# Output projection of a hybrid decoder step in two passes over the tokens, with the router's steps for the first 128 tokens inside the second pass

## The chip, the core and the metric

The kernel runs on one core of a Trainium2 chip. The core has TensorE (matrix products, written PE in the profile, its weight loads PEld), VectorE (DVE), ScalarE (ACT), GpSimd (POOL) and SyncE (SP), which here only issues transfers to 16 DMA engines. The engines run their own instruction streams and wait for each other on semaphores. The metric is the time of one execution on the device, in microseconds.

## What is computed

One inference step of a one-layer decoder trunk for 256 prompt tokens and 8 sampled tokens, 264 in all, width 1024: two recurrent branches, merged and projected by w_out, and then a mixture of 32 experts of which each token takes 4. All arithmetic is in 32-bit floats. What matters here is the end of the mixer and the mixture:

```python
merged = jax.nn.sigmoid(g_a) * branch_a + jax.nn.sigmoid(g_b) * branch_b
x = x + merged @ w_out                       # 1024 x 1024
u = rmsnorm(x, norm_ffn)
logits = u @ w_router + b_router             # 32 experts
top_v, top_i = lax.top_k(logits, TOP_K)      # TOP_K = 4
gates = jax.nn.softmax(top_v, axis=-1)
# for each expert e and its tokens xb:
gu = xb @ w_gate_up[e] + b_gate_up[e]        # 1024 x 2048
act = (up + 1.0) * (gate * jax.nn.sigmoid(SWIGLU_ALPHA * gate))
y = act @ w_down[e] + b_down[e]              # 1024 x 1024
```

The first two lines are written together here from the surrounding step; the rest is the reference's own. An expert has 12 MB of weights, all 32 have 384 MB (403 million bytes), and each is loaded once.

## The kernel before

**Layout.** Activations lie transposed: `xT` holds x as 8 tiles (`KT`) of 128 rows of the model width by 264 tokens. The tokens also come in three row tiles, `ROWS` = 128, 128 and 8 (the 8 sampled ones), called tile 0, 1 and 2 below. PSUM has eight banks, `ps[0]` to `ps[7]`; names such as `p_u`, `p_parts`, `p_logits` and `p_early` are the same eight banks in other roles.

**Output projection.** `project` (L1079) makes one output tile of 128 rows after the other. The w_out tiles are its last eight: 8 matmuls (k) of 128 x 128 weights against 264 columns, into `ps[0]` or `ps[1]` in turn. A matmul of this kind shows as two records in the trace, so a tile is 16 records. Its end raises `acc_ready` (89 to 96 for the w_out tiles; 88 marks the end of w_proj_b). VectorE adds the tile to `xT` (L1731) and raises `acc2_emptied`, for which TensorE waits before it uses that bank again. w_out lies in the four slots of `stream`, 256 columns each, and each slot is filled when w_proj_b's tile in it is done.

**Router.** TensorE forms partial products of `w_router` with `xT` (`logits_of`, four at a time side by side in the array, into `p_parts`) and turns `xT` into rows of tokens (`turn_u(t, h, js)`: token tile t, half h of the width, into `p_u`). ScalarE squares these rows (`square_u`, L790), takes the root (`root_u`, L797) and scales them (L809, `u_taken`). VectorE copies the partial products (L1765), TensorE sums them per token (`p_logits`), and VectorE runs, per token tile, scale and bias (L1743), the eight largest (L1745), cut to four (L1746, L1747), and the mark of chosen experts (L1752). From the marks, TensorE counts each token's rank at its expert (`p_rank0` for tile 0; `p_rank12` for tiles 1 and 2), VectorE makes a slot number (L1757) and a selection matrix `pick` (L1761), and TensorE gathers the first experts' inputs with it (`gather`). `keep_busy` is filler: matmuls whose results nobody reads.

**Experts.** They go in 16 pairs. A pair has six units of weights: four for gate and up, two for down, 4 MB each. There are five places for units in on-chip memory (`unit[0]` to `unit[4]`); place 3 is the memory of the four w_out slots, place 2 is free from `acc_ready` 88 on. SyncE issues the loads in the order of use; before it overwrites a place, it waits for `w_used`, which TensorE raises by one for each half unit (two k) that it has used. Ahead of the experts, SyncE's queue stands as in these lines, followed by the loads that wait for `w_used`:

```python
            sp.wait_ge(S["acc_ready"], 88)
            load_unit(0, 2, 2)
            sp.wait_ge(S["acc_ready"], 92)
            load_half(0, 3, 3, 0, unit_landed[3])
            sp.wait_ge(S["acc_ready"], 96)
            load_half(0, 3, 3, 1, half_landed[3])
            load_half(0, 4, 4, 1, half_landed[4])
```

The order of the work is written out by hand in each engine's block. Functions in the listing are those that the change touches and their callers.

## Time and profile before

| | us |
|---|---|
| median of 3 runs | 1379.17 (1378.71 to 1382.08) |
| the profiled execution | 1380.69 |
| its span in the trace | 1378.9 |
| TensorE busy, whole span | 1341.8 (97%) |
| VectorE busy | 417.9 (30%) |
| ScalarE busy | 260.3 (19%) |
| GpSimd busy | 38.9 (3%) |

By stretch of the span:

| stretch, us | what | TensorE busy | DMA share | GB/s |
|---|---|---|---|---|
| 325 to 415 | w_proj_a, w_proj_b | 89.87 of 90 | 0.82 | 259 |
| 415 to 457.5 | w_out, router | 40.95 of 42.5 | 0.81 | 325 |
| 457.5 to 1365 | experts | 883.28 of 907.5 | 0.99 | 422 |
| 1365 to 1378.9 | last sums, output | 7.21 of 13.9 | 0.21 | 78 |

The profile is one execution of the program. Busy time of matmuls includes modelled ends and so reaches over small gaps; where the spacing of matmuls matters, starts of successive rows are the better measure. The granted clock of TensorE was full (1.00) in most windows. A high busy share of TensorE and a DMA share of 0.99 stand side by side in the experts' stretch, so the shares alone don't say which one sets the pace.

### The profile page before, as it was taken

The page shows a single profiled execution, that of the slowest core. Times are in us where ns is not written, and L with a number is a line of the kernel's source. Part 1 is how long each engine was busy: PE and PEld are TensorE (multiplying, and loading weights), DVE is VectorE, ACT ScalarE, POOL GpSimd, SP SyncE. Part 2 cuts the span into 40 slices and gives each one's busy share as a digit, 9 for nine tenths or more (in the row PEclk, how much of TensorE's full clock was granted, in tenths as well). Part 3 has the DMA queues.
Part 4 walks back from the last instruction along what each step waited for, and adds up shares of the span by engine and source line. Part 5 has one row for each costly group of instructions (what it writes and reads, how often), then busy time and mean ns, then how long its engine had stood idle before and what let it go on. Part 6 is the DMA issues. An engine that isn't in the chain of part 4 may idle for free.

```text
span 1378.9 us, 16760 instructions
## 1 busy us (share of the span) xinstructions
PE 1341.8 (97%) x6864; PEld 746.5 (54%) x6864; DVE 417.9 (30%) x1089; ACT 260.3 (19%) x589; POOL 38.9 (3%) x58
## 2 busy tenths in 40 slices
PE   9999999999999999999999999999999989999998
PEld 8888878888888443443434444434334333434443
DVE  3754555887312321221122121211211211212112
ACT  2113273476200310110101101101011010101102
POOL 1000011210000000000000000000000000000000
PEclk9999999999999999999999999999999999999999
DMA  9444546898797899999999999999999999999995
GB/s 249 125 150 137 155 154 218 272 334 311 216 322 287 327 411 412 436 429 429 433 429 429 433 431 429 432 431 429 433 431 426 436 429 426 437 428 432 433 421 200
DMA packets 92549, 488.93 MB, mean 355 GB/s; under 512 B 8403, under 2 KB 72107, under 8 KB 76935
## 3 DMA queue, kind: packets, MB, share of 16 engines
q1 hardware_dynamic: 83560, 460.46, 82.6%
q0 software_dynamic: 4608, 24.41, 5.0%
q10 hardware_dynamic: 4306, 2.98, 0.8%
q8 instruction: 56, 0.92, 0.3%
q14 instruction: 19, 0.16, 0.0%
HBM read 476.91 MB, written 11.19 MB: 354 GB/s over the span
## 4 chain that ended last, share of the span: by engine, by line
PE 74%; DMA 21%; ACT 3%; DVE 1%; issue 0%; ACTq 0%; POOLq 0%; POOL 0%; SPq 0%; DVEq 0%
PE bank L310 72%; DMA ring<-in_w_gate_up 9%; DMA ring<-in_w_down 9%; DMA plain_conv<-in_w_down 3%; PE bank L914 2%; ACT ring L715 0%; ACT plain_conv L639 0%; ACT ring L677 0%; ACT ring L670 0%; DVE ring L1565 0%; DVE exn L1565 0%; ACT ring L665 0%; ACT ring L663 0%; DVE plain_conv L1562 0%; DVE ring L1562 0%
## 5 line engine op out<-in xcount | busy, mean ns | idle before, releaser
L310 PE MATMUL bank<-ring,plain_conv 128*64 128x512 f32 x1280 | 296.4, 605 | 7.6 <-DMA ring<-in_w_gate_up 7.6
L310 PE MATMUL bank<-exn,ring 128*128 128x264 f32 (+1 forms) x1168 | 265.9, 389 | 2.5 <-ACT plain_conv L611 2.3
L310 PEld LDWEIGHTS bank<-exn,ring 128*128 128x128 f32 (+1 forms) x1168 | 220.3, 190 | 44.6 <-issue 3.6
L310 PE MATMUL bank<-plain_conv 128*64 128x512 f32 (+2 forms) x848 | 186.7, 581 | 9.2 <-DMA plain_conv<-in_w_gate_up 8.8
L310 PEld LDWEIGHTS bank<-ring,plain_conv 128*64 128x64 f32 x1280 | 91.6, 139 | 187.3 <-issue 172.3
L310 PE MATMUL bank<-ring,exn 128*64 128x512 f32 x576 | 127.6, 595 | 3.3 <-DMA ring<-in_w_down 3.3
L310 PEld LDWEIGHTS bank<-plain_conv 128*64 128x64 f32 (+1 forms) x848 | 63.0, 140 | 123.8 <-issue 107.3
L1806 DVE TENSOR_TENSOR xT<-xT,bank 128x264 f32<-128x264 f32 x128 | 55.0, 430 | 222.7 <-PE bank L310 221.0
L1812 DVE TENSOR_SCALAR bank<-bank 128x512 f32<-128x512 f32 x31 | 21.7, 700 | 316.7 <-PE bank L310 316.7
L310 PE MATMUL bank<-plain_conv,exn 128*64 128x512 f32 (+1 forms) x422 | 99.9, 590 | 1.2 <-DMA plain_conv<-in_w_down 0.9
L823 ACT ACTIVATE exn<-bank 128x512 f32<-128x512 f32 x31 | 18.5, 598 | 413.8 <-DVE bank L1812 413.8
L310 PEld LDWEIGHTS bank<-rstd,exn 128*128 128x128 f32 (+2 forms) x772 | 76.9, 190 | 15.9 <-issue 13.0
L310 PE MATMUL bank<-rstd,exn 128*128 128x128 f32 (+2 forms) x772 | 83.7, 280 | 0.2 <-DVE rstd L1761 0.2
L310 PEld LDWEIGHTS bank<-ring,exn 128*64 128x64 f32 x576 | 40.2, 137 | 77.3 <-issue 72.1
L310 PE MATMUL bank<-ring 128*128 128x264 f32 (+3 forms) x520 | 80.4, 336 | 0.0
L310 PEld LDWEIGHTS bank<-ring 128*128 128x128 f32 (+1 forms) x520 | 67.8, 170 | 13.3 <-issue 4.8
L828 ACT COPY exn<-bank 128x512 f32<-128x512 f32 x31 | 18.2, 587 | 256.6 <-PE bank L914 250.3
L310 PEld LDWEIGHTS bank<-plain_conv,exn 128*64 128x64 f32 (+1 forms) x422 | 31.4, 137 | 59.6 <-issue 56.5
L310 PE MATMUL bank<-rstd,plain_conv 128*128 128x264 f32 x256 | 61.2, 392 | 0.0
L310 PEld LDWEIGHTS bank<-rstd,plain_conv 128*128 128x128 f32 x256 | 47.3, 190 | 20.3 <-issue 13.0
L310 PE MATMUL bank<-plain_conv,ring 128*128 128x264 f32 x256 | 57.8, 387 | 0.1
L1693 DVE TENSOR_TENSOR plain_conv<-bank,small 128x512 f32<-128x512 f32 x15 | 10.4, 692 | 146.6 <-PE bank L310 146.6
(294 smaller groups left out, 865.3 us busy)
## 6 DMA issues: line engine op xcount, KB each, us to landing
ring<-in_w_gate_up SPq DMA_DIRECT2D x35, 4096.0 KB, 38.0
plain_conv<-in_w_gate_up SPq DMA_DIRECT2D x23, 4096.0 KB, 39.8
ring<-in_w_down SPq DMA_DIRECT2D x16, 4096.0 KB, 39.2
plain_conv<-in_w_down SPq DMA_DIRECT2D x11, 4096.0 KB, 37.5
ring<-in_w_in SPq DMA_DIRECT2D x36, 1024.0 KB, 5.3
ring<-in_w_gate_up SPq DMA_DIRECT2D x8, 2048.0 KB, 10.9
ring<-in_w_down SPq DMA_DIRECT2D x5, 2048.0 KB, 9.1
ring<-in_w_proj_b SPq DMA_DIRECT2D x8, 1024.0 KB, 8.8
```

The source lines that it names most:

```text
L310: return nc.tensor.matmul(out, w, x, start=start, stop=stop)
L823: nc.scalar.activation(h_act, gate, ACT.Sigmoid, scale=1.702).then_inc(S["sg_ready"], 1)
L828: nc.scalar.copy(to.rearrange("p c s -> p (c s)"), bank[:, :]).then_inc(S["ht_ready"], 1)
L914: return nc.tensor.transpose(out, src, ident[0:k, 0:k])
L1693: done("xt_left", V.tensor_tensor(xt[:, 0:4, :], bank[:, :].rearrange("p (k s) -> p k s", k=4), n_ffn_x[:, 0:4].unsqueeze(2).to_broadcast( ...
L1806: done("comb_emptied", V.tensor_tensor(xT[:, c, :], xT[:, c, :], p_comb[c % 4][:, 0:NT], ALU.add))
L1812: V.tensor_scalar(g_last if last else gate, gate, 7.0, None, ALU.min).then_inc(S["g1_ready"], 1)
```

## The change

w_out's eight output tiles are made twice (`project_out(u)`, u = 0 to 15): in pass one over the first 128 tokens, in pass two over the other 136. `acc_ready` and `acc2_emptied` count eight more. `logits_of` takes a column range. Tile 0's router steps (partial products, turns, squares, root, logits, mark, ranks, pick, scaling) stand between the tiles of pass two on TensorE, VectorE and ScalarE; after pass two, tiles 1 and 2 go through the same steps, written in pairs. Some PSUM roles move to other banks. The gather of tile 0 for the first experts stands ahead of the ranks of tiles 1 and 2, one of the two filler blocks is gone, the other stands behind that gather. SyncE waits for `acc_ready` 100 and 104 where it waited for 92 and 96. The cut diff:

```diff
@@ -285,7 +285,7 @@
-        p_parts, p_logits, p_rank0, p_rank12, p_early = ps[5], ps[0], ps[1], ps[2], ps[0]
+        p_parts, p_logits0, p_logits, p_rank0, p_rank12, p_early = ps[5], ps[4], ps[1], ps[7], ps[2], ps[0]
@@ -394,9 +394,9 @@
             load_half(0, 4, 4, 0, unit_landed[4])
             sp.wait_ge(S["acc_ready"], 88)
             load_unit(0, 2, 2)
-            sp.wait_ge(S["acc_ready"], 92)
+            sp.wait_ge(S["acc_ready"], 100)
             load_half(0, 3, 3, 0, unit_landed[3])
-            sp.wait_ge(S["acc_ready"], 96)
+            sp.wait_ge(S["acc_ready"], 104)
             load_half(0, 3, 3, 1, half_landed[3])
...
@@ -786,29 +786,39 @@
...
+            square_u(0, 0)
+            square_u(0, 1)
+            root_u(0)
+            scale_u(0, 0)
+            scale_u(0, 1)
+            square_u(1, 0)
+            square_u(2, 0)
+            for t in range(1, 3):
                 square_u(t, 1)
                 root_u(t)
             for h in range(2):
-                for t, n in enumerate(ROWS):
-                    act.wait_ge(S["rstd_ready"], t + 1)
-                    scaled = u_tok[t][0:n, 512 * h:512 * h + 512] if t < 2 else us[32 * h:32 * h + n, :]
-                    nc.scalar.activation(scaled.rearrange("n (s p) -> n s p", s=4),
-                                         p_u[t][h][0:n, :].rearrange("n (p s) -> n s p", s=4), ACT.Copy,
-                                         scale=rstd_u[0:n, t:t + 1]).then_inc(S["u_taken"], 1)
+                for t in range(1, 3):
+                    scale_u(t, h)
...
+            def project_out(u):
+
+                half, t = u // KT, u % KT
+                cols = other_cols if half else first_cols
+                if half == 0 and t % 2 == 0:
+                    pe.wait_ge(landed[t // 2], 16 * 12 + 16)
+                pe.wait_ge(S["acc2_emptied"], KT - 1 + u)
+                for k in range(KT):
+                    if u == 0:
+                        pe.wait_ge(S["merged_ready"], k + 1)
+                    w = stream[t // 2][:, 256 * k + P * (t % 2):256 * k + P * (t % 2) + P]
+                    ins = mm(ps[u % 2][:, cols], w, plain[:, GA + k, cols], k == 0, k == KT - 1)
+                ins.then_inc(S["acc_ready"], 1)
+
             pe.wait_ge(emptied["s"], sum(w == "s" for _, w in uses))
             pe.wait_ge(emptied["v"], sum(w == "v" for _, w in uses))
-            for t in range(KT):
-                project(12, KT, lambda k: plain[:, GA + k, :], 16, t, t + 1, ready=lambda k: (S["merged_ready"], k + 1))
-                if t == 5:
-                    pe.wait_ge(S["acc2_emptied"], KT + 4)
-                    pe.wait_ge(S["router_set"], 2)
-                    logits_of(range(4))
-                    for w in range(3):
-                        turn_u(w, 0, range(4))
-            pe.wait_ge(S["acc2_emptied"], 2 * KT - 1)
-            turn_u(0, 1, range(3))
-            turn_u(1, 1, range(3))
+            for u in range(KT + 1):
+                project_out(u)
             pe.wait_ge(S["acc2_emptied"], 2 * KT)
-            turn_u(0, 1, [3])
-            logits_of(range(4, KT)).then_inc(S["parts_filled"], 1)
-            turn_u(1, 1, [3])
+            pe.wait_ge(S["router_set"], 2)
+            logits_of(range(KT), first_cols).then_inc(S["parts_filled"], 1)
+            turn_u(0, 0, range(4))
+            project_out(KT + 1)
+            turn_u(0, 1, range(4))
             pe.wait_ge(S["parts_taken"], 1)
-            for t, n in enumerate(ROWS):
-                ins = mm(p_logits[0:n, E * t:E * t + E], parts[:, P * t:P * t + n], one_of[:, 0:E], True, True)
-            ins.then_inc(S["logits_filled"], 1)
-            turn_u(2, 1, range(4))
-            keep_busy(p_rank0, 2)
+            turn_logits(p_logits0, [0])
+            for u in range(KT + 2, KT + 5):
+                project_out(u)
             pe.wait_ge(S["mark_ready"], 1)
             mm(p_rank0[:, 0:E], before[:, :], mark[:, 0, :], True, True).then_inc(S["rank0_filled"], 1)
+            project_out(KT + 5)
+            pe.wait_ge(S["acc2_emptied"], 2 * KT + 4)
+            logits_of(range(4), other_cols)
+            for w in range(1, 3):
+                turn_u(w, 0, range(4))
+            for u in range(KT + 6, 2 * KT):
+                project_out(u)
+            pe.wait_ge(S["pick0_ready"], 1)
+            pe.wait_ge(S["acc2_emptied"], 3 * KT - 1)
+            turn_u(1, 1, range(3))
+            pe.wait_ge(S["acc2_emptied"], 3 * KT)
+            turn_u(1, 1, [3])
+            logits_of(range(4, KT), other_cols).then_inc(S["parts_filled"], 1)
+            pe.wait_ge(S["parts_taken"], 2)
+            turn_logits(p_logits, (1, 2))
+            turn_u(2, 1, range(4))
             pe.wait_ge(S["u_taken"], 2)
-            keep_busy(p_first[0], 2)
-            pe.wait_ge(S["mark_ready"], 2)
-            mm(p_rank12[:, 0:E], ones[:, :], mark[:, 0, :], True, False).then_inc(S["fin_filled"], 5)
-            mm(p_rank12[:, 0:E], before[:, :], mark[:, 1, :], False, True)
-            mm(p_rank12[0:TS, E:2 * E], ones[:, 0:TS], mark[:, 0, :], True, False)
-            mm(p_rank12[0:TS, E:2 * E], ones[:, 0:TS], mark[:, 1, :], False, False)
-            mm(p_rank12[0:TS, E:2 * E], before[0:TS, 0:TS], mark[0:TS, 2, :], False, True).then_inc(S["rank12_filled"], 1)
 
...
-            pe.wait_ge(S["u_taken"], 3)
-            for t in range(3):
+            gather(p_early, range(2), [0])
+            keep_busy(p_rank12, 2)
+            pe.wait_ge(S["mark_ready"], 2)
+            mm(p_rank12[:, 0:E], ones[:, :], mark[:, 0, :], True, False).then_inc(S["fin_filled"], 5)
+            mm(p_rank12[:, 0:E], before[:, :], mark[:, 1, :], False, True)
+            mm(p_rank12[0:TS, E:2 * E], ones[:, 0:TS], mark[:, 0, :], True, False)
+            mm(p_rank12[0:TS, E:2 * E], ones[:, 0:TS], mark[:, 1, :], False, False)
+            mm(p_rank12[0:TS, E:2 * E], before[0:TS, 0:TS], mark[0:TS, 2, :], False, True).then_inc(S["rank12_filled"], 1)
+            pe.wait_ge(S["u_taken"], 4)
+            for t in range(1, 3):
                 pe.wait_ge(S["pick0_ready"], t + 1)
                 ins = gather(p_early, range(2), [t])
             ins.then_inc(S["early_filled"], 1)
@@ -1726,24 +1767,38 @@
...
-            for t in range(KT):
-                dve.wait_ge(S["acc_ready"], 88 + t + 1)
-                V.tensor_tensor(xT[:, t, :], xT[:, t, :], ps[t % 2][:, 0:NT], ALU.add).then_inc(S["acc2_emptied"], 1)
-                if t == KT - 2:
-                    for w, n in enumerate(ROWS):
-                        dve.wait_ge(S["usq_ready"], w + 1)
-                        done("part_ready", V.tensor_scalar(ssq_p[0:n, w:w + 1], ssq_h[0:n, w, 0:1], 1.0 / D, EPS, ALU.mult, ALU.add))
-
+            def add_out(u):
+
+                cols = slice(P, NT) if u >= KT else slice(0, P)
+                dve.wait_ge(S["acc_ready"], 88 + u + 1)
+                V.tensor_tensor(xT[:, u % KT, cols], xT[:, u % KT, cols], ps[u % 2][:, cols], ALU.add).then_inc(S["acc2_emptied"], 1)
...
@@ -1761,18 +1816,47 @@
...
+            for u in range(KT + 1):
+                add_out(u)
             dve.wait_ge(S["parts_filled"], 1)
-            done("parts_taken", V.tensor_copy(parts, p_parts[:, 0:NT]))
+            done("parts_taken", V.tensor_copy(parts[:, 0:P], p_parts[:, 0:P]))
+            add_out(KT + 1)
+            mean_square(0, 1)
+            add_out(KT + 2)
+            token_scale(0)
+            dve.wait_ge(S["rstd_ready"], 1)
             dve.wait_ge(S["logits_filled"], 1)
-            link(token_logits(0))
+            link(token_logits(0, p_logits0))
+            link(token_top(0))
+            add_out(KT + 3)
+            link(V.memset(top[:, 0, TOPK:8], LOWEST))
+            link(token_left(0))
             mark_tokens(0, 1)
-            link(token_logits(1))
-            link(token_logits(2))
-            mark_tokens(1, 2)
-            dve.wait_ge(S["mark_ready"], 2)
+            add_out(KT + 4)
             dve.wait_ge(S["rank0_filled"], 1)
             link(place_tokens(0, p_rank0[:, 0:E]))
             pick_first(0)
+            for u in range(KT + 5, 2 * KT - 1):
+                add_out(u)
+            mean_square(1, 3)
+            mean_square(2, 4)
+            add_out(2 * KT - 1)
+            dve.wait_ge(S["parts_filled"], 2)
+            done("parts_taken", V.tensor_copy(parts[:, P:NT], p_parts[:, P:NT]))
+            token_scale(1)
+            dve.wait_ge(S["rstd_ready"], 2)
+            dve.wait_ge(S["logits_filled"], 2)
+            link(token_logits(1, p_logits))
+            link(token_top(1))
+            token_scale(2)
+            dve.wait_ge(S["rstd_ready"], 3)
+            link(token_logits(2, p_logits))
+            link(token_top(2))
+            link(V.memset(top[:, 1:3, TOPK:8], LOWEST))
+            token_left(1)
+            link(token_left(2))
+            mark_tokens(1, 2)
+            dve.wait_ge(S["mark_ready"], 2)
             dve.wait_ge(S["rank12_filled"], 1)
             place_tokens(1, p_rank12[:, 0:E])
             place_tokens(2, p_rank12[0:TS, E:2 * E])
```

What stands in a row on the engines shows the same at three places. The rows give the line, the operation, the result and what it is made of, and its size as rows by columns. On TensorE w_out's matmuls are those on plain_conv,ring; those on xT,exn are the router's partial products; those on ident,xT are turns. Before, from the start of w_out:

```order
L310 MATMUL bank<-plain_conv,ring 128x264 x48
L310 MATMUL bank<-xT,exn 32x264 x4
L914 MATMUL bank<-ident,xT 128x128 x8
L914 MATMUL bank<-ident,xT 8x128 x4
L310 MATMUL bank<-plain_conv,ring 128x264 x16
```

After, from the same place:

```order
L310 MATMUL bank<-plain_conv,ring 128x128 x64
L310 MATMUL bank<-plain_conv,ring 128x136 x8
L310 MATMUL bank<-xT,exn 32x128 x8
L924 MATMUL bank<-ident,xT 128x128 x4
L310 MATMUL bank<-plain_conv,ring 128x136 x8
L924 MATMUL bank<-ident,xT 128x128 x4
L310 MATMUL bank<-plain_conv,exn 128x32
L310 MATMUL bank<-plain_conv,ring 128x136 x24
L310 MATMUL bank<-plain_conv,before 128x32
L310 MATMUL bank<-plain_conv,ring 128x136 x8
L310 MATMUL bank<-xT,exn 32x136 x4
L924 MATMUL bank<-ident,xT 128x128 x4
```

The 64 matmuls of 264 columns have become 64 of 128 and 64 of 136, and router work of tile 0 stands between the latter.

TensorE, from the last w_out matmuls on, before (slot_no,ident is filler, before and ones are the triangles and ones of the rank sums, rstd,exn the gather):

```order
L310 MATMUL bank<-xT,exn 32x264 x4
L914 MATMUL bank<-ident,xT 128x128
L310 MATMUL bank<-plain_conv,exn 128x32 x2
L310 MATMUL bank<-plain_conv,exn 8x32
L914 MATMUL bank<-ident,xT 8x128 x4
L310 MATMUL bank<-slot_no,ident 128x320 x2
L310 MATMUL bank<-plain_conv,before 128x32
L310 MATMUL bank<-slot_no,ident 128x320 x2
L310 MATMUL bank<-plain_conv,ones 128x32
L310 MATMUL bank<-plain_conv,before 128x32
L310 MATMUL bank<-plain_conv,ones 8x32 x2
L310 MATMUL bank<-plain_conv,before 8x32
```

After, from the last 16 matmuls of w_out:

```order
L310 MATMUL bank<-plain_conv,ring 128x136 x16
L924 MATMUL bank<-ident,xT 128x128 x4
L310 MATMUL bank<-xT,exn 32x136 x4
L310 MATMUL bank<-plain_conv,exn 128x32
L310 MATMUL bank<-plain_conv,exn 8x32
L924 MATMUL bank<-ident,xT 8x128 x4
L310 MATMUL bank<-rstd,exn 128x128 x2
L310 MATMUL bank<-slot_no,ident 128x320 x2
L310 MATMUL bank<-plain_conv,ones 128x32
L310 MATMUL bank<-plain_conv,before 128x32
L310 MATMUL bank<-plain_conv,ones 8x32 x2
L310 MATMUL bank<-plain_conv,before 8x32
```

Tile 0's logits and ranks are gone from here, its gather stands ahead of the ranks, and one filler block is left.

VectorE, from the last add into xT on, before:

```order
L1731 TENSOR_TENSOR xT<-xT,bank 128x264
L1765 COPY exn<-bank 128x264
L1741 RECIPROCAL exn<-exn 128x1
L1743 SCALAR_TENSOR_TENSOR exn<-bank,exn,small 128x32
L1745 MAX plain_conv<-exn 128x8
L1746 MEMSET plain_conv 128x4
L1747 MATCH_REPLACE exn<-plain_conv,exn 128x36
L1752 TENSOR_TENSOR plain_conv<-exn 128x32
L1741 RECIPROCAL exn<-exn 128x1
L1743 SCALAR_TENSOR_TENSOR exn<-bank,exn,small 128x32
L1745 MAX plain_conv<-exn 128x8
L1746 MEMSET plain_conv 128x4
```

After, from the last add of pass two:

```order
L1774 TENSOR_TENSOR xT<-xT,bank 128x136
L1845 COPY exn<-bank 128x136
L1786 RECIPROCAL exn<-exn 128x1
L1791 SCALAR_TENSOR_TENSOR exn<-bank,exn,small 128x32
L1797 MAX plain_conv<-exn 128x8
L1786 RECIPROCAL exn<-exn 8x1
L1791 SCALAR_TENSOR_TENSOR exn<-bank,exn,small 8x32
L1797 MAX plain_conv<-exn 8x8
L1855 MEMSET plain_conv 128x2x4
L1802 MATCH_REPLACE exn<-plain_conv,exn 128x36
L1802 MATCH_REPLACE exn<-plain_conv,exn 8x36
L1807 TENSOR_TENSOR plain_conv<-exn 128x64
```

Three rounds of scale, maximum and replacement (the third begins below the first list) have become two, of which the second has 8 rows, with one memset for both.

## Rows read from the trace of the kernel before

**Rows 1.** Windows: from:to, length, busy us (records) by engine, PEclk, DMA share, GB/s
```profile
440.00:445.00 5.00, 5.00 (x24) 4.29 (x23) 0.60 (x4) 0.00 (x0) 0.00 (x0) 1.00 0.07 23
...
455.00:460.00 5.00, 5.00 (x30) 2.93 (x31) 2.78 (x7) 0.00 (x0) 0.00 (x0) 1.00 0.46 193
...
600.00:700.00 100.00, 100.00 (x527) 41.92 (x523) 19.57 (x38) 10.76 (x24) 0.00 (x0) 1.00 1.00 431
```

**Rows 2.** Chain that ended last: start, length in us, what
```profile
843.83 37.53 DMA plain_conv<-in_w_down
```

**Rows 3.** SyncE's queue in time, 385 to 600 us: start, length from first to last, issue
```profile
429.67 16.62 SPq L367 DMA_DIRECT2D ring<-in_w_gate_up  x2
...
461.20 6.98 SPq L367 DMA_DIRECT2D ring<-in_w_down  x2
473.75 3.76 SPq L367 DMA_DIRECT2D plain_conv<-in_w_gate_up  x2
```

**Rows 4.** Timeline, TensorE, 405 to 475 us: start, length, line, operation, records
```profile
415.24 21.52 PE L310 MATMUL bank<-plain_conv,ring 128*128 128x264 f32 x96
...
436.69 0.66 PE L310 MATMUL bank<-xT,exn 128*32 128x264 f32 x8
...
438.64 7.29 PE L310 MATMUL bank<-plain_conv,ring 128*128 128x264 f32 x32
...
446.71 0.65 PE L310 MATMUL bank<-xT,exn 128*32 128x264 f32 x8
...
457.50 3.65 PE L310 MATMUL bank<-ring,plain_conv 128*64 128x512 f32 x16
```

**Rows 5.** Timeline, VectorE, ScalarE and TensorE around the router, 405 to 475 us
```profile
418.42 0.23 DVE L1709 COPY plain_conv<-plain_conv 128x128 f32<-128x128 f32 x1
...
445.97 0.43 DVE L1731 TENSOR_TENSOR xT<-xT,bank 128x264 f32<-128x264 f32 x1 [2.96 <-PE bank L310]
...
448.94 0.25 DVE L1743 SCALAR_TENSOR_TENSOR exn<-bank,exn,small 128x32 f32<-128x32 f32 x1
...
449.27 0.59 ACT L790 ACTIVATE plain_conv<-bank 8x512 f32<-8x512 f32 x1 [0.42 <-PE bank L914]
...
450.05 0.29 ACT L797 ACTIVATE exn<-exn 8x1 f32<-8x1 f32 x1
...
451.53 1.34 PE L310 MATMUL bank<-slot_no,ident 128*128 128x320 f32 x4 [1.00 <-ACT exn L809]
...
452.19 0.23 DVE L1752 TENSOR_TENSOR plain_conv<-exn 128x64 f32<-128x64 f32 x1
...
452.71 0.30 PE L310 MATMUL bank<-plain_conv,ones 128*128 128x32 f32 x2
```

**Rows 6.** Short matmuls: weight loads 213 to 224 us, timeline 145 to 180, group 330 to 520
```profile
218.14 0.19 PEld L310 LDWEIGHTS bank<-ring 128*128 128x128 f32 x1 [0.24 <-issue]
...
220.78 0.19 PEld L310 LDWEIGHTS bank<-ring 128*128 128x128 f32 x1 [0.24 <-issue]
...
167.87 4.53 PE L914 MATMUL bank<-ident,plain_conv 128*128 128x128 f32 x40
172.24 1.95 PE L310 MATMUL bank<-plain_conv 128*128 128x128 f32 x16
174.12 0.61 PE L310 MATMUL bank<-rstd,exn 32*128 32x8 f32 x4
...
L310 PE MATMUL bank<-rstd,exn 128*128 128x128 f32 x64 | 8.5, 283 | 0.2 <-DVE rstd L1761 0.2
```

**Rows 7.** The four loads of w_out, by tensor
```profile
DMA to landing us min/median/max: 5.0/6.5/10.4
```

**Rows 8.** Timeline, TensorE, 870 to 905 and 1005 to 1025 us: the same eight records
```profile
898.99 1.09 PE L310 MATMUL bank<-exn,plain_conv 32*64 32x512 f32 x8
...
1020.51 1.98 PE L310 MATMUL bank<-exn,plain_conv 32*64 32x512 f32 x8 [2.84 <-issue]
```

More of the change, by code:

```diff
@@ L1127, in turn_u, with turn_logits @@
                     ins.then_inc(S["u_filled"], 1)
+            def turn_logits(bank, ts):
+                for t in ts:
+                    n = ROWS[t]
+                    ins = mm(bank[0:n, E * t:E * t + E], parts[:, P * t:P * t + n], one_of[:, 0:E], True, True)
+                ins.then_inc(S["logits_filled"], 1)
             def keep_busy(bank, n):
@@ L1194, in _ @@
             LEFT, RIGHT = range(4), range(4, KT)
-            pe.wait_ge(S["u_taken"], 3)
-            for t in range(3):
+            gather(p_early, range(2), [0])
[8 more added lines that the diff above has]
+            for t in range(1, 3):
                 pe.wait_ge(S["pick0_ready"], t + 1)
```

38 lines of the change are left out of this document (26 added, 12 removed).

## Prediction

> **What bounds the kernel now.** I read the windows of DMA traffic first. Between 600 and 700 us the 16 DMA engines are busy 100% of the time at 431 GB/s while they bring in expert weights, whereas just ahead there are holes: 23 GB/s in 440 to 445 us, 193 GB/s in 455 to 460 us [rows 1]. The chain that ended last agrees for the late part: from 843.83 us it passes again and again through weight transfers of some 40 us each, 37.53 the first, which is how long a 4 MB unit queues behind others [rows 2]. So from about 470 us to the tail the kernel takes "bytes still to load, divided by 431 GB/s", and its end moves only if the last hole in the DMA traffic moves.
>
> Which hole is the last? SyncE's issues answer it. After the first five units are asked for, the next 2 MB is issued at 461.2 us and another 6.98 us later (the row merges the two), the one after at 473.75 us [rows 3]. Each of these waits for TensorE to use up a half unit (w_used). 2 MB (2.1 million bytes) at 431 GB/s take 4.9 us and the second of them is issued 7 us after the first, so up to 468 us TensorE paces the transfers; later issues come before the queue is empty. Hence what counts is the start of the first expert matmul, 457.50 us [rows 4]. Everything between the start of w_out (415.24 us) and 457.50 us is TensorE work and the router's latency, and it moves the end one for one. Transfers before 457 us have slack: the halves issued near 446 us are 4.2 million bytes, 9.7 us of traffic, gone by 457 us, and nobody needs them before the second half of the first expert pair.
>
> **The stretch to be rebuilt.** w_out's 64 matmuls show as 128 TensorE records of 264 columns: 96 in 415.24 to 436.69, 32 from 438.64; one costs 21.45 / 96 = 0.2234 us, so the last one ends at 438.64 + 32 x 0.2234 = 445.79 us [rows 4]. Call that point Z. Then: VectorE's last add 445.97 to 446.40; router partial products from 446.71; the tokens' chain on VectorE from 448.94, ending with the mark of tiles 1 and 2 at 452.19 + 0.23 = 452.42; the ranks' first matmul 452.71 [rows 4, 5]. Z to ranks is 6.92 us, ranks to first expert matmul 4.79 us.
>
> **Part 1, w_out in two passes.** The same columns (128 + 136 = 264) go through in twice as many matmuls: 256 records for 128. What a record of 128 columns costs is shown by other places. In the final-state stage the weight loads repeat every 220.78 - 218.14 = 2.64 us, for 16 records of 128 columns and 2 of 512; with 0.43 for each of the two (half of the 0.85 that 512 columns would need by 0.2234 x 512 / 264 = 0.433), (2.64 - 0.86) / 16 = 0.111 us [rows 6]. The CB products: 16 records from 172.24 to the next row at 174.12, 0.1175 us. A bare share of the 264-column record would be 0.2234 x 128 / 264 = 0.108. I take 0.1115, since that row comes from a stage with changing full-size weights and accumulating pairs as here; for 136 columns 0.1115 + 8 x 0.00085 = 0.1183. Sum: 128 x 0.1115 + 128 x 0.1183 = 29.41 us, against 128 x 0.2234 = 28.60 us: **+0.8 us** (bounds: +0.0 at the bare share, +2.4 at 0.1175 and 0.1243).
>
> First-pass banks are also emptied twice as often. VectorE ends its router set-up at 418.42 + 0.23 = 418.65 us [rows 5], and tile 2 of pass one would like to start at 415.24 + 32 x 0.1115 = 418.81 us. It needs add 0, which starts at 418.65 and takes between 0.23 us (a copy of 128 columns) and 0.43 us (the add of 264) [rows 5]; I take 0.28 for 128 or 136 columns. **+0.2 us** stall, once; each later tile takes 1.78 us on TensorE against one short add. The bounds are 0 and 0.4.
>
> **Part 2, router work inside pass two.** What now stands on TensorE between 415.24 us and the new Z: the old 8 partial-product records and 12 turns took 438.64 - 436.69 = 1.95 us [rows 4]; 12 turns at (172.24 - 167.87) / 40 = 0.109 us are 1.31, the products 0.6 [rows 6]. New: products of all 8 k for the first 128 columns (16 records of 128, the same columns as 8 of 264) 0.6; products of 4 k for 136 columns 0.3; turns: 4 + 4 for tile 0, 8 for tiles 1 and 2's left half, 16 x 0.109 = 1.75; tile 0's logits and its ranks 0.25 each, as in the short rows of the tail. Sum 3.15, so **+1.2 us**. No stall is added there: between two adds VectorE has 1.9 us and the pieces put there (a reciprocal, a scaled add, a max; or a place and a pick) are under 1 us; the waits that TensorE meets (parts_taken, mark_ready 1, pick0_ready) follow at least one whole tile after their inputs. ScalarE's two squares, root and two scalings of tile 0 also fall under the tiles. If that cover failed, each stall would cost at most a tile's 1.9 us.
> New Z = 445.79 + 0.8 + 0.2 + 1.2 = 448.0 us, 2.2 later.
>
> **Part 3, the tail after Z.** The last add has 136 columns: 0.15 shorter. Copy: 0.15 shorter. Partial products 136 instead of 264 columns wide: 0.2 shorter. Logits: 4 records instead of 6, but VectorE now waits for the root of tile 1, which needs ScalarE's square and root after the last turn: turn done Z + 0.9, square 0.78, root 0.29: Z + 1.95, early enough; logits of tile 1 start at Z + 2.3, where the old tile 0 started at 448.94 = Z + 3.15. Old: three tiles of about 1.1 us each, in a row. New: logits and max of tile 1 (0.5), then tile 2 waits for its own root: turn of tile 2 done Z + 2.75, square and root as before from 449.27 to 450.34 = 1.07, so Z + 3.85 [rows 5]; then reciprocal, logits, max 0.7, memset and two replacements 0.7, mark 0.25: mark ends at Z + 5.5. Before it ended at Z + 6.63, and a block of filler matmuls (451.53, 1.34 long) still held the ranks for 0.2 us; the new filler follows earlier and is over. Ranks at Z + 5.6: **-1.3 us**. So ScalarE's root of the 8-row tile is what comes late next, not VectorE's arithmetic. From the ranks to the experts nothing changes but 4 gather records of tile 0, which stood in the shadow of picks of tile 1 and are now done before: 0. Scaling of tiles 1 and 2 (4 instead of 6 instructions, from Z + 3.85 on) is done by Z + 6.3, before the gather and the experts need it.
>
> **Part 4, transfers.** SyncE's waits go from acc_ready 92 and 96 to 100 and 104. The first half of unit 3 leaves at about 439 us instead of 429.67, the rest at 448 instead of 446. Queued behind them on SyncE is only the issue of 461 us. 9.7 us after 448 plus the 1 us of start is 459, still ahead of it: 0. Pass one asks for the last w_out slot at 426 us instead of 436.7; it is issued at 415.4 us and the four loads of w_out land 5.0 to 10.4 us after their issue [rows 7], so even the slowest would be there at 425.8: 0.
>
> **Sum:** +2.2 - 1.3 = +0.9, rounded **+1.0 us** at the first expert matmul (458.5 us) and at the end: span 1379.9 for 1378.9, profiled time 1381.7 for 1380.69; the median of the runs was 1379.17, 1.5 below the profiled run, and gives 1380.2. A measurement of this kernel cannot tell less than about 0.3% (4.1 us) from no change.
>
> **Where a rule speaks against the change.** The row on the 128-column stream shows 0.111 us a record, 4 ns over its share [rows 6]. The Trainium skill, TensorE: Matmul & The Clock Gate, "Back-to-back issue gap", says that in a stream of weight-load and matmul pairs the spacing at 128 columns is about 81 ns where the matmul alone would be 56, some 25 ns more for the load. By it, as an estimate, 256 records would cost 6.4 us more, and the time would be near 1385.
>
> **Rivals.**
> (a) The columns cost only their share and the tail gains as worked out: +0.0 for part 1, no stall; total -0.1; with the tail's waits on ScalarE hidden too (0.8 less) -1: **1378.5**.
> (b) Slower: short matmuls don't hide their weight loads. For it speaks the group of gather records, 64 records of 128 x 128 with 8.5 us busy, 0.133 us each [rows 6]; against it the 0.111 and 0.1175. At 0.133 and 0.141 part 1 would be 35.1 - 28.6 = +6.5 rather than +0.8: **1386**. It decides from 0.127 us a record on, where the whole reaches +4.1.
> (c) The sparser TensorE tail lets the clock fall as the experts start. It was at full in the windows read here [rows 1]; later, where TensorE waited 2.84 us for data, 8 records took 1.98 us right after, against 1.09 elsewhere [rows 8]. One group of 16 records (3.65) at half clock adds up to 3.65: **1384**. Against it: waits here are under 1 us each and one filler block is left.
> (d) The end doesn't follow the first expert matmul, since the queue has slack that I don't see: 0, **1379.2**.
> (e) The 128 first tokens' steps release something earlier that I missed and the tail shrinks by over 4 us: only possible if the 4.79 us after the ranks shrank too; nothing in the order says so: **1374**.
>
> **How the numbers follow.** Forecast 0.58; (a) 0.15; (b) 0.10; (c) 0.07; (d) 0.06; (e) 0.04. Faster by over 0.3% (below 1375.0): only (e), 0.04. Slower by over 0.3% (above 1383.3): (b) and half of (c), 0.13. Within: 0.83. The likeliest case alone spans 1378.9 to 1382.2 with the bounds of part 1. The range takes in (a), (d) and most of (c), 1377.5 to 1384.5, leaving (b), (e) and the rest of (c) outside.
>
> **What would show it.** In the new profile: records of 128 columns 0.11 apart (part 1); last w_out matmul ending near 448 us (parts 1, 2); mark to ranks at about 5.6 us after it (part 3); first expert matmul near 458.5 us, next weight issue near 462 us, and the DMA hole before it shorter though the one before that is longer (part 4). If the first expert matmul starts before 456 or after 461 us, my sum is wrong; if it starts near 458.5 and the end still moves by more than 3 us, my bound is wrong.

## The result and the profile after

The changed kernel took 1386.29 us (median of 7 runs, 1383.07 to 1390.73), the kernel before 1380.49 us (7 runs, 1378.71 to 1384.68). The ratio is 1.0036, 95% interval 1.0025 to 1.0047: 5.0 us slower, 3.5 to 6.5. The forecast was 1380.2, its range 1377.5 to 1384.5.

The profiled execution of the changed kernel has a span of 1381.3 us, only 2.4 more than before. That number misleads. In both kernels everything ahead of w_out is the same, yet w_out starts at 415.24 us in the one profile [rows 4] and at 413.29 us in the other:

```profile
413.29 8.90 PE L310 MATMUL bank<-plain_conv,ring 128*128 128x128 f32 x76
```

The reason, for about 1.7 of these 1.95 us, is a stretch in which TensorE's granted clock stood at half in the first profile alone (PEclk 0.75 in 42 to 46 us and 0.82 in 46 to 50; 1.00 in both in the other). Windows of the kernel before, then of the changed one, from to, length, busy by engine, PEclk, DMA share, GB/s:

```profile
42.00:46.00 4.00, 4.00 (x39) 3.56 (x38) 2.89 (x8) 0.00 (x0) 0.00 (x0) 0.75 0.85 258
```

```profile
42.00:46.00 4.00, 4.00 (x39) 3.68 (x38) 3.19 (x9) 0.00 (x0) 0.00 (x0) 1.00 0.82 261
```

So I don't compare spans below but **M**, the time from w_out's first matmul to SyncE's first load that the experts release. It is 461.20 - 415.24 = 45.96 us before [rows 3, 4]. After, SyncE's queue reads (start, length from first to last, issue):

```profile
437.27 9.36 SPq L367 DMA_DIRECT2D ring<-in_w_gate_up  x2
...
463.69 6.97 SPq L367 DMA_DIRECT2D ring<-in_w_down  x2
476.24 3.76 SPq L367 DMA_DIRECT2D plain_conv<-in_w_gate_up  x2
```

M is 463.69 - 413.29 = 50.40 us, 4.4 us more, which is close to the 5.0 of the timed runs. The next issues keep the same distance (476.24 - 463.69 = 12.55 us, as 473.75 - 461.20 before), so all of it is lost by then.

Where? The timeline of TensorE in the changed kernel, the tail of w_out and the router up to the experts:

```profile
429.79 0.65 PE L310 MATMUL bank<-xT,exn 128*32 128x128 f32 x16
...
433.29 5.81 PE L310 MATMUL bank<-plain_conv,ring 128*128 128x136 f32 x48
...
438.94 0.30 PE L310 MATMUL bank<-plain_conv,before 128*128 128x32 f32 x2
...
442.41 3.87 PE L310 MATMUL bank<-plain_conv,ring 128*128 128x136 f32 x32
...
449.17 1.24 PE L310 MATMUL bank<-slot_no,ident 128*128 128x320 f32 x4
451.71 0.38 PE L310 MATMUL bank<-plain_conv,ones 128*128 128x32 f32 x2 [1.31 <-DVE plain_conv L1807]
...
453.74 3.69 PE L310 MATMUL bank<-rstd,exn 128*128 128x128 f32 x20 [1.06 <-DVE rstd L1816]
...
457.35 6.29 PE L310 MATMUL bank<-ring,plain_conv 128*64 128x512 f32 x16
...
463.57 3.13 PE L310 MATMUL bank<-rstd,exn 128*128 128x128 f32 x24
```

VectorE's mark of tiles 1 and 2, after:

```profile
451.34 0.23 DVE L1807 TENSOR_TENSOR plain_conv<-exn 128x64 f32<-128x64 f32 x1
```

TensorE's gather and the row behind the first expert matmuls, before:

```profile
454.50 3.07 PE L310 MATMUL bank<-rstd,exn 128*128 128x128 f32 x20 [0.25 <-DVE rstd L1761]
...
461.08 3.13 PE L310 MATMUL bank<-rstd,exn 128*128 128x128 f32 x24
```

Up to the ranks all is as forecast. Pass one and the first tile of pass two are over at 429.79, 16.50 us after the start (16.4 by the sum: 128 x 0.1115 + 0.2 + 16 x 0.1183). The 48 records from 433.29 take 5.65 us to the next row at 438.94, 0.118 each, and the last w_out matmul ends at 442.41 + 32 x 0.118 = 446.2 us, 32.9 after the start (30.55 before, 32.8 forecast). The mark stands at 451.34 and the ranks at 451.71, 5.5 us after that end. Then comes what was not forecast: the 20 gather records take 3.61 us to the next row's start, where they took 3.00 before, and the first 16 expert records take 6.22 us to the next row against 3.58 before (457.50 [rows 4] to 461.08). TensorE ran at its lower level, 1.2 GHz of 2.4:

```profile
450.00:452.00 2.00, 0.69 (x5) 0.32 (x3) 1.27 (x9) 1.97 (x4) 0.00 (x0) 1.00 0.97 418
452.00:454.00 2.00, 0.94 (x11) 0.74 (x11) 1.12 (x7) 0.40 (x1) 0.00 (x0) 1.00 0.96 410
454.00:456.00 2.00, 2.00 (x16) 1.74 (x15) 1.01 (x5) 0.00 (x0) 0.00 (x0) 0.97 1.09 467
456.00:458.00 2.00, 2.00 (x8) 1.22 (x8) 0.42 (x1) 0.00 (x0) 0.00 (x0) 0.50 0.74 311
458.00:460.00 2.00, 2.00 (x8) 0.50 (x6) 1.59 (x2) 0.00 (x0) 0.00 (x0) 0.50 0.00 0
...
462.00:464.00 2.00, 2.00 (x9) 0.66 (x6) 0.00 (x0) 0.00 (x0) 0.00 (x0) 0.83 0.00 0
```

Before the clock fell, TensorE was busy 0.69 of 2 us and 0.94 of 2 us in the windows from 450 and 452, waiting 1.31 us for the mark ahead of the ranks and 1.06 us for the picks behind them, as the rows at 451.71 and 453.74 show. In the profile before, at the same distance from w_out's start (windows from 452 and 454 us), it was busy 2.00 and 1.75 of 2 us.

Loss at half clock: 0.61 + 2.64 = 3.25 us. Without it M would be 47.15, +1.2, where +1.0 was forecast.

### The profile page after: what moved, and what is told of

The parts are those of the page before. It is cut to its first block, busy times and chain, and to the rows that moved or that the text cites. A ratio compares the mean times of both kernels' runs of the same rounds, so it can differ in the third digit from the quotient of the medians.

```text
span 1381.3 us, 17051 instructions
## 1 busy us (share of the span) xinstructions
PE 1340.0 (97%) x7004; PEld 749.6 (54%) x7004; DVE 418.8 (30%) x1097; ACT 260.3 (19%) x589; POOL 39.0 (3%) x58
## 3 DMA queue, kind: packets, MB, share of 16 engines
q10 hardware_dynamic: 4306, 2.98, 0.8%
## 4 chain that ended last, share of the span: by engine, by line
PE 73%; DMA 21%; ACT 3%; DVE 1%; ACTq 1%; issue 1%; POOLq 0%; POOL 0%; SPq 0%; DVEq 0%
PE bank L310 72%; DMA ring<-in_w_down 9%; DMA ring<-in_w_gate_up 6%; DMA plain_conv<-in_w_gate_up 3%; DMA plain_conv<-in_w_down 3%; PE bank L924 2%; DMA plain_conv<-in_norm_mix 0%; ACT ring L715 0%; ACT plain_conv L639 0%; ACT ring L677 0%; ACT ring L670 0%; DVE ring L1606 0%; DVE exn L1606 0%; ACT ring L665 0%; ACT ring L663 0%
## 5 line engine op out<-in xcount | busy, mean ns | idle before, releaser
L310 PE MATMUL bank<-plain_conv,ring 128*128 128x264 f32 (+2 forms) x384 | 59.3, 314 | 0.1
L310 PEld LDWEIGHTS bank<-plain_conv,ring 128*128 128x128 f32 x384 | 53.8, 191 | 5.3 <-issue 1.1
```

Source lines behind the costliest of these rows:

```text
L310: return nc.tensor.matmul(out, w, x, start=start, stop=stop)
```

## Experiments

Each is compared with 21 to 29 runs of the kernel before on the same chip, whose medians are 1380.42 to 1381.33 us; the change itself with the 7 above. The expectations call "clock theory" the reading just given: TensorE's waits in the router's tail let its clock fall over the gather and the first expert matmuls. "Filler a + b" means filler matmuls between the end of w_out and the ranks of tiles 1 and 2, and behind those ranks. Waits are TensorE's in the tail, as its timeline shows them, added up. Waits, clock and M come from the one profiled execution of each kernel, ratio and range from the timed runs.

| kernel | passes | filler | waits, us | clock at the experts' start | M, us | ratio, 95% interval | lowest, highest run |
|---|---|---|---|---|---|---|---|
| before | 1 | 4 + 0 | 1.55 | full | 45.96 | | |
| e4_late_load | 1 | 4 + 0 | 1.55 | full | 45.96 | 1.0003, 0.9994 to 1.0012 | 1378.77, 1382.81 |
| e3_bare | 1 | 0 | 3.13 | half | 50.64 | 1.0036, 1.0022 to 1.0049 | 1384.25, 1387.88 |
| the change | 2 | 2 + 0 | 2.79 | half | 50.40 | 1.0036, 1.0025 to 1.0047 | 1383.07, 1390.73 |
| e1_again | 2 | 2 + 0 | 2.78 | half | 50.40 | 1.0037, 1.0023 to 1.0051 | 1385.54, 1387.14 |
| e2_filled | 2 | 5 + 1 | 0.74 | full | 47.18 | 1.0015, 1.0006 to 1.0024 | 1380.54, 1385.23 |
| e5_two_pass | 2 | 4 + 0 | 1.54 | full | 46.76 | 1.0015, 1.0006 to 1.0024 | 1379.69, 1384.26 |
| e8_fill_ahead | 2 | 5 + 0 | 1.48 | half | 50.46 | one run | 1386.02 |
| e13_fill_ahead_timed | 2 | 5 + 0 | 1.48 | half | 50.46 | 1.0029, 1.0020 to 1.0038 | 1382.84, 1386.38 |
| e9_fill_behind | 2 | 2 + 1 | 2.04 | full | 47.12 | 1.0017, 1.0003 to 1.0032 | 1379.95, 1388.24 |
| e10_gather_back | 2 | 2 + 0 | 2.59 | half | 50.38 | 1.0033, 1.0020 to 1.0046 | 1381.24, 1389.40 |
| e7_two_pass_early_turn | 2 | 4 + 1 | 0.32 | full | 46.31 | 1.0009, 1.0000 to 1.0018 | 1378.71, 1383.37 |
| e6_one_pass_paired | 1 | 4 + 0 | 0.86 | full | 45.42 | 1.0003, 0.9994 to 1.0012 | 1378.25, 1382.58 |
| e11_paired_short | 1 | 3 + 0 | 0.61 | half | 49.57 | 1.0016, 1.0001 to 1.0030 | 1378.18, 1386.93 |
| e12_paired_moved_fill | 1 | 4 + 0 | 0.45 | full | 45.16 | 0.9997, 0.9988 to 1.0006 | 1378.16, 1382.23 |

### Does the fall come back?

The changed kernel, unedited.

> The changed kernel once more, for its spread. Measure M: from w_out's first matmul to SyncE's first load released by the experts; 45.96 us before, 50.40 us in the profile of the change. Clock theory: of these 4.4 us some 3.4 come from TensorE running at half clock over the first expert matmuls; if that happens in every execution, the granted clock shows a half-clock stretch at about 456 to 463 us again, M near 50.4, time +4 to +6 us against before. If it depends on chance, M is near 47 in executions without it. Rival (late loads of place 3): M near 47 and the time lost in the experts' stretch.

Measured: M 50.40 again, half clock again, 1386.42 us for 1381.33. The fall came in both profiles, and all 5 timed runs are at 1385.54 or above. This profile has the early half-clock stretch too: w_out starts at 415.88 us and the span is 1385.1.

### Fill the waits, and nothing else

```diff
             gather(p_early, range(2), [0])
-            keep_busy(p_rank12, 2)
+            keep_busy(p_rank12, 5)
...
             mm(p_rank12[0:TS, E:2 * E], before[0:TS, 0:TS], mark[0:TS, 2, :], False, True).then_inc(S["rank12_filled"], 1)
+            keep_busy(ps[6], 1)
```

> The change with TensorE's waits in the router tail filled: 5 filler matmuls instead of 2 ahead of the ranks of tiles 1 and 2, and 1 after them. Clock theory: no half-clock stretch at the start of the experts, M = 50.4 - 3.4 = 47.0, time +1 us against before (within 0.1%). Rival (the two passes and the extra router work cost 4 to 5 us by themselves, or the late loads do): M may fall but the time stays at +4 to +6 us.

Measured: M 47.18, the clock theory's number, and a ratio of 1.0015, 2.1 us (0.8 to 3.3) where about 1 was expected. Four more filler matmuls, work without a result, take 3.2 us out of M and, by the medians of runs made side by side, 3.15 us out of the time (1386.42 to 1383.27). TensorE's timeline shows the gather at 2.98 us to the next row and the first expert records at 3.58:

```profile
451.14 2.86 PE L310 MATMUL bank<-slot_no,ident 128*128 128x320 f32 x10
...
455.78 3.04 PE L310 MATMUL bank<-rstd,exn 128*128 128x128 f32 x20 [0.32 <-DVE rstd L1817]
458.76 3.65 PE L310 MATMUL bank<-ring,plain_conv 128*64 128x512 f32 x16
462.34 3.13 PE L310 MATMUL bank<-rstd,exn 128*128 128x128 f32 x24
```

What is left, 1.2 us in M and some 2 us in time, is what the change costs by itself.

### Take the filler from the kernel before

```diff
             turn_u(2, 1, range(4))
-            keep_busy(p_rank0, 2)
...
             pe.wait_ge(S["u_taken"], 2)
-            keep_busy(p_first[0], 2)
```

> The kernel before with both of its filler blocks taken away and nothing else. Clock theory: TensorE waits some 2.4 us more in the tail, the clock falls at the start of the experts, M = 45.96 + 2.5 to 3.5, time +2.5 to +4 us. Rival (the fall has to do with the narrow matmuls of the two passes, not with the tail's waits): clock stays full, M 45.8, no change in time.

Measured: the kernel before without its filler is as slow as the changed one, 1.0036, M 50.64. Neither passes nor narrow matmuls are needed for the fall. It came sooner and lasted longer:

```profile
450.00:452.00 2.00, 0.49 (x2) 0.36 (x2) 1.68 (x11) 1.91 (x6) 0.00 (x0) 0.69 1.11 475
452.00:464.00 12.00, 11.01 (x42) 7.73 (x44) 5.71 (x22) 2.29 (x4) 0.00 (x0) 0.50 0.47 199
```

```profile
450.56 0.49 PE L310 MATMUL bank<-plain_conv,before 128*128 128x32 f32 x2 [0.89 <-DVE plain_conv L1750]
452.99 0.60 PE L310 MATMUL bank<-plain_conv,ones 128*128 128x32 f32 x2 [1.94 <-DVE plain_conv L1750]
...
454.46 6.49 PE L310 MATMUL bank<-rstd,exn 128*128 128x128 f32 x24
460.88 5.38 PE L310 MATMUL bank<-ring,plain_conv 128*64 128x512 f32 x16
466.19 3.13 PE L310 MATMUL bank<-rstd,exn 128*128 128x128 f32 x24
```

The 24 gather records take 6.42 us, the first expert records 5.31. The price was above the expected +2.5 to +3.5 in M, as the gather was hit whole. Ranks start at 452.99 - 415.67 = 37.32 us after w_out's start, slightly sooner than the 37.47 before, so the filler cost 0.15 us there.

### Load place 3 later

```diff
-            sp.wait_ge(S["acc_ready"], 92)
+            sp.wait_ge(S["acc_ready"], 96)
             load_half(0, 3, 3, 0, unit_landed[3])
```

> The kernel before with the first half of place 3 loaded only after all of w_out (acc_ready 96 instead of 92), 16 us later, twice the delay that the change brings it. If loads ahead of the first released one have slack, M stays 46 and the time moves by less than 1 us, although the traffic queued at 446 us is then 6.3 million bytes or 14.6 us, ending at the very moment (461 us) at which the first released load is issued. Rival (late loads cost the 5 us): +3 us or more.

Measured: M 45.96, ratio 1.0003. Transfers now run on in 455 to 460 us (share 0.99, 0.46 before [rows 1]), and the experts start no later:

```profile
443.80 0.80 SPq L367 DMA_DIRECT2D ring<-in_w_gate_up  x2
...
459.04 6.98 SPq L367 DMA_DIRECT2D ring<-in_w_down  x2
```

```profile
455.00:460.00 5.00, 5.00 (x29) 2.35 (x28) 2.84 (x7) 0.00 (x0) 0.00 (x0) 1.00 0.99 423
```

So the later waits of SyncE in the change are not the cause.

### The two passes alone

`project_out` as in the change, for u = 0 to 15, with the router's steps of the kernel before at their places: the first part behind the sixth tile, now of pass two, the rest behind the last. SyncE waits for 100 and 104, as in the change:

```diff
-            for t in range(KT):
-                project(12, KT, lambda k: plain[:, GA + k, :], 16, t, t + 1, ready=lambda k: (S["merged_ready"], k + 1))
-                if t == 5:
-                    pe.wait_ge(S["acc2_emptied"], KT + 4)
...
+            for u in range(2 * KT):
+                project_out(u)
+                if u == KT + 5:
+                    pe.wait_ge(S["acc2_emptied"], 2 * KT + 4)
                     pe.wait_ge(S["router_set"], 2)
                     logits_of(range(4))
```

> Two passes alone: w_out in 128 and 136 columns, all router steps after them as in the kernel before, both filler blocks kept, loads of place 3 at acc_ready 100 and 104. By my sum the passes cost 0.8 us of columns and 0.2 us of stall and the last add is 0.15 us shorter: last w_out matmul 1.0 us later, M = 46.8, clock full, time +0.9 us (not to be told from before). Rival (the narrow matmuls are what costs): M 48 or more.

Measured: M 46.76, +0.80. The short matmuls hide their weight loads and cost what the 0.111 us row said: in the changed kernel the records are 0.112 us apart at 128 columns and 0.118 at 136. The ratio, 1.0015, is 2.1 us, with an interval from 0.8 to 3.3, so the part above M's 0.8 is not explained by M.

### Which wait?

Filler ahead of the ranks only (`keep_busy(p_rank12, 5)`), in one execution (e8), then in eleven (e13):

> The change with 5 fillers instead of 2 ahead of the ranks, none behind them. Which of TensorE's two waits lets the clock fall, the 1.31 us ahead of the ranks or the 1.06 us behind? If the first alone or the sum of both decides, the clock stays full and M is 47.0; if the one behind the ranks decides, the clock falls and M is 50.4.

> The change with 5 fillers ahead of the ranks and none behind, as in the one look at it (fall in the profile, M 50.45), now timed. If the wait behind the ranks lets the clock fall in every execution, the time is +4 to +6 us against before and the runs lie in one group like those of the change. If the fall happens by chance there, as with one filler behind the ranks, the times spread from +0 to +6 us in two groups.

Filler behind the ranks only (the line on `ps[6]` of e2_filled):

> The change with one filler matmul behind the ranks of tiles 1 and 2 and nothing else. The run with filler only ahead of the ranks kept the fall (M 50.45), so the 1.06 us wait behind the ranks is needed for it. If it alone decides: clock full, M 47.2, time +1 to +2 us against before. If both waits together decide: the clock still falls, M 50.4.

The gather of tile 0 back behind the ranks, no filler added:

```diff
-            gather(p_early, range(2), [0])
             keep_busy(p_rank12, 2)
...
             mm(p_rank12[0:TS, E:2 * E], before[0:TS, 0:TS], mark[0:TS, 2, :], False, True).then_inc(S["rank12_filled"], 1)
+            gather(p_early, range(2), [0])
```

> The change with the gather of tile 0 put back behind the ranks, where the kernel before had it; no filler added. It stands in the same 1.06 us wait, so if that place decides: clock full, M 47.2 (the gather costs nothing, since its picks are waited for anyway). If what counts is the total of work in the tail, which is unchanged here: the clock falls, M 50.4.

Measured: filling the first wait alone changes nothing, twice M 50.46, and all 11 timed runs are at 1382.84 or above:

```profile
449.19 2.86 PE L310 MATMUL bank<-slot_no,ident 128*128 128x320 f32 x10
...
453.84 3.90 PE L310 MATMUL bank<-rstd,exn 128*128 128x128 f32 x20 [1.06 <-DVE rstd L1816]
457.67 6.07 PE L310 MATMUL bank<-ring,plain_conv 128*64 128x512 f32 x16
463.67 3.13 PE L310 MATMUL bank<-rstd,exn 128*128 128x128 f32 x24
```

One filler matmul behind the ranks (e9) gave a profile at full clock, M 47.12:

```profile
456.35 3.04 PE L310 MATMUL bank<-rstd,exn 128*128 128x128 f32 x20 [0.32 <-DVE rstd L1817]
459.33 3.65 PE L310 MATMUL bank<-ring,plain_conv 128*64 128x512 f32 x16
```

But its ten timed runs reach from 1379.95 to 1388.24. I read them as executions with and without the fall, since the filled kernel's lie within 5 us; no profile of a slow one was taken, so this is not shown. With the gather there instead (e10), the wait behind the ranks is down to 0.42 us as well, but the one ahead of them is 1.75, and the profile shows the fall:

```profile
454.08 0.38 PE L310 MATMUL bank<-plain_conv,ones 128*128 128x32 f32 x2 [1.75 <-DVE plain_conv L1807]
...
456.11 4.34 PE L310 MATMUL bank<-rstd,exn 128*128 128x128 f32 x20 [0.42 <-DVE rstd L1816]
460.38 5.61 PE L310 MATMUL bank<-ring,plain_conv 128*64 128x512 f32 x16
```

Its runs spread from 1381.24 to 1389.40, most of them high. So my expectation that this one place decides is half wrong: with the place behind the ranks left open the clock fell both times (e8, e13), and with it covered it fell in one profile (e10) and not in another (e9).

### Router tail of one pass, paired

One pass as before. The vector steps of tiles 0 and 1 are paired, and the turns of the 8-row tile go ahead of the logits into bank 1 (the ranks of tile 0 go to bank 5):

```diff
-        p_u = [[ps[2], ps[6]], [ps[3], ps[7]], [ps[4], ps[5]]]
+        p_u = [[ps[2], ps[6]], [ps[3], ps[7]], [ps[4], ps[1]]]
...
             turn_u(1, 1, [3])
+            turn_u(2, 1, range(4))
             pe.wait_ge(S["parts_taken"], 1)
...
+            token_scale(0)
             dve.wait_ge(S["logits_filled"], 1)
-            link(token_logits(0))
+            dve.wait_ge(S["rstd_ready"], 1)
+            token_logits(0)
+            token_scale(1)
+            dve.wait_ge(S["rstd_ready"], 2)
+            link(token_logits(1))
+            token_top(0)
+            link(token_top(1))
...
             mark_tokens(0, 1)
-            link(token_logits(1))
...
```

> One pass over all 264 tokens as before, but the tail's vector steps of tiles 0 and 1 paired and the turns of the 8-row tile made ahead of the logits, into another bank, so that its square and root don't come last. Both filler blocks kept. If the tail before was bound by three vector rounds in a row and by ScalarE's last root, the mark of tiles 1 and 2 comes about 1.0 us earlier: M = 45.0, time -1 us, clock full. Rival (what is paired only waits elsewhere): M 45.8 to 46; or the shorter activity lets the clock fall and M is 48.

The same with the second filler block cut:

```diff
-            keep_busy(p_first[0], 2)
+            keep_busy(p_first[0], 1)
```

> One pass with the paired tail, second filler block of 1 instead of 2, since in the run before that block ended 0.4 us after the mark and held up the ranks. If so M = 45.41 - 0.35 = 45.05, time -0.9 us against before, too little to be told from it. If the shorter filler lets the clock fall: M 48 or more, time +2 us or more.

And with that matmul put into the first block:

```diff
-            keep_busy(p_rank0, 2)
+            keep_busy(p_rank0, 3)
```

> One pass, paired tail, filler moved: 3 matmuls in the first block and 1 in the second instead of 2 and 2. With 2 and 1 the clock fell in the profile (M 49.56) and the times lay in two groups. If the filler taken from the second block may as well stand in the first, where TensorE waits 0.4 us anyway, the clock stays full, M = 45.1 and the times lie in one group, time -0.9 to 0 us against before. If the place counts, the clock falls as before: M 49.5.

Measured: M 45.42, then 49.57, then 45.16. With one filler matmul less (e11), and no wait longer than 0.40 us, the clock fell in the profile; with that matmul moved into the block ahead (e12) it didn't. The timed runs agree: of e11's 12, six are at 1381.71 or below and six at 1384.49 or above, while e12's 11 all lie between 1378.16 and 1382.23. Timelines, e11, then e12:

```profile
448.80 1.34 PE L310 MATMUL bank<-slot_no,ident 128*128 128x320 f32 x4
450.54 0.41 PE L310 MATMUL bank<-plain_conv,before 128*128 128x32 f32 x2 [0.40 <-DVE plain_conv L1760]
451.16 0.81 PE L310 MATMUL bank<-slot_no,ident 128*128 128x320 f32 x2 [0.21 <-ACT exn L809]
...
452.91 6.48 PE L310 MATMUL bank<-rstd,exn 128*128 128x128 f32 x24
459.32 5.61 PE L310 MATMUL bank<-ring,plain_conv 128*64 128x512 f32 x16
```

```profile
446.96 1.88 PE L310 MATMUL bank<-slot_no,ident 128*128 128x320 f32 x6
...
449.32 0.81 PE L310 MATMUL bank<-slot_no,ident 128*128 128x320 f32 x2 [0.20 <-ACT exn L809]
...
452.03 3.07 PE L310 MATMUL bank<-rstd,exn 128*128 128x128 f32 x20 [0.25 <-DVE rstd L1769]
455.03 3.65 PE L310 MATMUL bank<-ring,plain_conv 128*64 128x512 f32 x16
```

e12 has the shortest M of all, 0.8 us less than before, and a ratio of 0.9997 (0.9988 to 1.0006): it is ahead of the changed kernel and can't be told from the kernel before. Nor can e6, whose M is 0.5 us shorter and whose ratio is 1.0003.

### The same early turns in two passes

The change with filler 4 + 1 (the one behind on `ps[1]`) and:

```diff
-        p_u = [[ps[2], ps[6]], [ps[3], ps[7]], [ps[4], ps[5]]]
+        p_u = [[ps[2], ps[6]], [ps[3], ps[7]], [ps[4], ps[6]]]
...
-            pe.wait_ge(S["parts_taken"], 2)
-            turn_logits(p_logits, (1, 2))
-            turn_u(2, 1, range(4))
             pe.wait_ge(S["u_taken"], 2)
+            turn_u(2, 1, range(4))
+            pe.wait_ge(S["parts_taken"], 2)
+            turn_logits(p_logits, (1, 2))
```

> The change with filler (4 ahead of the ranks, 1 behind) and the turns of the 8-row tile made ahead of the logits into a bank that is free by then. Filled alone gave M 47.18. My reading is that ScalarE's root of that tile comes last after the change; then the mark is 0.7 to 0.8 us earlier and M = 46.4, time +0.5 us. Rival (VectorE's arithmetic bounds the tail): M 47.1.

Measured: M 46.31. After the change the root of the 8-row tile was indeed what came last. VectorE waited 1.15 us for it in the change and 0.23 us in e7:

```profile
450.09 0.15 DVE L1786 RECIPROCAL exn<-exn 8x1 f32<-8x1 f32 x1 [1.15 <-ACT exn L797]
```

```profile
449.15 0.15 DVE L1787 RECIPROCAL exn<-exn 8x1 f32<-8x1 f32 x1 [0.23 <-ACT exn L797]
```

Making its turns early gives 0.87 us of M against e2_filled (which has one filler matmul more ahead of the ranks), and the best form of the change that was run is still 0.35 us behind the kernel before in M, 1.0009 (1.0000 to 1.0018) in time.

## Why the prediction was wrong

- **The bound held.** The end follows the first load that the experts release. Over all the profiles, M and the timed ratios rise together: M up to 1.2 us longer than before, or shorter, goes with ratios from 0.9997 to 1.0017, M 3.6 to 4.7 us longer with 1.0016 to 1.0037 (1.0016 is e11, where half of the runs lie low). Traffic ahead of it has slack, as part 4 said (e4). Behind it all 15 profiles run alike at first: for 409 us from the first released load on, SyncE's issues lie within 0.02 us of the kernel before's. Only then do transfers stand in TensorE's way, from 843.83 us in the kernel before [rows 2].
- **Part 1 right.** +0.8 + 0.2 us forecast, +0.80 in M measured with the add's gain in it (e5); rival (b) is out, the records are 0.112 and 0.118 us apart. The rule of the Trainium skill that was weighed there (TensorE: Matmul & The Clock Gate, "Back-to-back issue gap"), with an estimated 6.4 us, does not hold for this stream.
- **Parts 2 and 3 right in size.** Last w_out matmul +2.3 us (2.2 forecast); ranks 5.5 us after it (5.6). "ScalarE's root of the 8-row tile is what comes late next" is shown by VectorE's wait for it and by e7.
- **The step that failed** is rival (c), put at 0.07 and dismissed with "waits here are under 1 us each and one filler block is left". I had the mark and the ranks in my sum but didn't lay TensorE's own work against them: its filler would be over about 1.3 us before the mark came, and behind the ranks the gather of tile 0 no longer stood in the wait for the picks. The waits are 1.31 and 1.06 us. "The new filler follows earlier and is over", written down as a gain of 0.2 us, and "now done before: 0" for the moved gather, were the two places where the cover went. Its price was right: 3.65 us as a bound, 3.25 us measured, and its 1384 would have been nearer than my forecast.
- **"From the ranks to the experts nothing changes"**, 4.79 us, was wrong by the clock: 5.64 us (457.35 - 451.71), 0.61 of it half-clock gather, 0.24 a later pick.
- **The range** reached to 1384.5, just past rival (c) by itself. What came is M's 4.4 us, 0.6 us that the timed runs show beyond M, and a kernel before that reads 1380.49 in 7 runs instead of 1379.17 in 3, so 1.3 of the 6.1 us between forecast and median are no effect of the change.
- **The rest beyond M** (0.6 us for the change, 0.9 in e2, 1.3 in e5, where M's 0.8 lies at the edge of the interval) arises late. From the first released load to the end of the span the profiles take 917.4 to 919.6 us, and all of this difference comes after the 409 us in which they run alike. The mean is 917.8 us for the six profiles of one pass and 918.6 for the nine of two passes. Whether the two passes cause that, with one profile each, is open.
- **Slips of the working that change nothing:** rival (b) would decide from 0.123 us a record of 128 columns on, not 0.127 (0.127 is the mean of both sizes there). The bounds of part 1 alone span 1379.3 to 1381.7, not 1378.9 to 1382.2. The last w_out slot was asked for at 438.64 us before, not 436.7. The 2.84 us ahead of the slow eight records have no wait for data in their row, which says "issue".

What stays open: what sets the fall in each case. It is shown that it costs 3 to 5 us, that taking filler away brings it (e3, e11) and that with filler in both places it is absent from the profiles (e2, e7). It is not shown by what rule: the sum of waits doesn't order the cases (0.61 us with the fall in e11, 1.55 without it before).

## What to carry to other kernels

Where a step moves work away from an engine whose clock depends on its activity, list what that engine does in the gaps that are left, and price the clock as a term of the sum, not as a remark: here moving router work under other work brought the ranks 1.4 us closer to the last w_out matmul, the extra work ahead of that matmul cost 2.3, and the quieter tail lost 3.3 more. Ahead of a stretch that paces everything after it, filler is part of the schedule; when matmuls are moved out of a wait, put filler in their place and check the granted clock in several executions. Compare two profiles from a common event onward, not by their spans.

## What was not expected of the hardware

- A half-clock stretch in the windows of 42 to 50 us, behind small transposes that follow w_in's first matmuls (40 records of 24 x 24 from 41.36 us), comes in some executions and not in others of the same instructions, and shifts the start of w_out: 413.08 to 413.56 us in the profiles without it, 415.24 to 415.95 us in those that have it. The stretch itself costs about 1.7 us (0.75 and 0.82 of full clock over 4 us each in the kernel before), over a third of the effect looked for here.
- Records of 512 and of 128 columns both slow down with the clock: 16 expert records took 6.22 us instead of 3.58, the last of them with the clock on its way back, and 24 gather records, all at half clock (e3), 6.42 instead of some 3.1.
- With one filler matmul fewer and no wait above 0.40 us, TensorE's clock could fall (e11), and with that matmul placed earlier it stayed full in the profile (e12).
